# A third seven-product block in each down projection of a two-layer decoder trunk

## The reference

```python
h = rms_norm(x, g_ffn_pre)
f = jax.nn.silu(jnp.einsum('bsd,df->bsf', h, w_gate)) * jnp.einsum('bsd,df->bsf', h, w_up)
x = x + rms_norm(jnp.einsum('bsf,fd->bsd', f, w_down), g_ffn_post)
```

## Time and profile before

| | us |
|---|---|
| runs shown: median (lowest to highest) | 569.01 (568.5 to 569.04) |
| the profiled execution's own time | 568.8 |
| its span, first to last instruction | 567.0 |
| TensorE busy | 559.4 |
| DVE busy | 406.0 |
| ScalarE busy | 301.0 |
| POOL busy | 258.7 |

### The profile page before, as it was taken

The page is one execution under the profiler, slowest core; times in us unless marked ns, Lnnn a source line. Parts: engine busy times, 40 slices in busy tenths (PEclk is TensorE's granted clock), DMA queues, the critical chain, the costliest instruction groups (busy, mean ns, idle before and its releaser), DMA issues.

```text
span 567.0 us, 8931 instructions
## 1 busy us (share of the span) xinstructions
PE 559.4 (99%) x3383; PEld 460.1 (81%) x3383; DVE 406.0 (72%) x529; ACT 301.0 (53%) x428; POOL 258.7 (46%) x451
## 2 busy tenths in 40 slices
PE   8999999999999999999999999999999999999996
PEld 5878878888888888888888878888888888888884
DVE  5799895946755566777797987776848556395783
ACT  7576684664445354354546748564645454345530
POOL 1101001507697787994230000133296797879901
PEclk9999999999999999999999999999999999999999
DMA  8954624538565553547475443526575554644601
GB/s 304 378 203 161 232 94 169 224 133 312 186 223 180 191 213 127 180 174 262 168 266 184 164 168 108 228 76 222 223 260 174 197 202 144 249 148 149 214 10 74
DMA packets 18731, 107.35 MB, mean 189 GB/s; under 512 B 2816, under 2 KB 3072, under 8 KB 7168
## 3 DMA queue, kind: packets, MB, share of 16 engines
q1 hardware_dynamic: 18688, 106.78, 51.6%
HBM read 105.72 MB, written 1.05 MB: 188 GB/s over the span
## 4 chain that ended last, share of the span: by engine, by line
PE 92%; DVE 5%; ACT 1%; issue 1%; POOL 0%; DVEq 0%; POOLq 0%
PE bank L1398 78%; PE bank L1475 4%; PE bank L1413 3%; DVE w_l L919 3%; PE bank L1460 2%; PE bank L1501 2%; PE bank L1528 2%; PE bank L1469 1%; ACT work L725 0%; ACT w_h L642 0%; DVE work L981 0%; DVE work L1003 0%; DVE x L1081 0%; DVE work L1004 0%; DVE work L1074 0%
## 5 line engine op out<-in xcount | busy, mean ns | idle before, releaser
L919 DVE TENSOR_TENSOR w_l<-raw,w_h 128x2048 fp32r<-128x2048 f32 (+1 forms) x90 | 204.4, 2276 | 71.4 <-ACT w_h L642 71.1
L591 POOL COPY work<-work 32x128 f32<-32x128 f32 (+1 forms) x384 | 217.7, 567 | 78.3 <-DVE work L1120 62.5
L1398 PE MATMUL bank<-w_h,actT_h 128*128 128x512 f32 (+1 forms) x568 | 223.9, 394 | 0.3 <-DVE work L981 0.3
L1398 PE MATMUL bank<-w_h,actT_l 128*128 128x512 f32 (+1 forms) x568 | 219.9, 387 | 0.0
L1398 PE MATMUL bank<-w_l,actT_h 128*128 128x512 f32 (+1 forms) x568 | 219.4, 386 | 0.0
L642 ACT ACTIVATE w_h<-raw 128x2048 fp32r<-128x2048 f32 (+1 forms) x90 | 169.6, 1895 | 65.8 <-PE bank L1398 57.5
L1398 PEld LDWEIGHTS bank<-w_h,actT_h 128*128 128x128 f32 x568 | 106.8, 188 | 23.5 <-issue 2.8
L1398 PEld LDWEIGHTS bank<-w_h,actT_l 128*128 128x128 f32 x568 | 106.6, 188 | 22.2
L1398 PEld LDWEIGHTS bank<-w_l,actT_h 128*128 128x128 f32 x568 | 106.9, 188 | 20.0
L576 POOL TENSOR_TENSOR norms<-norms,constants 128x1 f32<-128x1 f32 x8 | 2.7, 342 | 129.0 <-ACT bank L752 129.0
L1475 PE MATMUL bank<-ident,work 128*128 128x128 f32 x228 | 31.4, 273 | 0.0
(11 more groups left out here) (113 smaller groups left out, 566.8 us busy)
## 6 DMA issues: line engine op xcount, KB each, us to landing
raw<-in_w_blocks SPq DMA_DIRECT2D x90, 1024.0 KB, 4.8
gains<-in_b_in SPq DMA_DIRECT2D x8, 256.0 KB, 5.9
raw<-in_w_blocks SPq DMA_DIRECT2D x4, 256.0 KB, 5.5
raw<-in_w_blocks SPq DMA_DIRECT2D x2, 512.0 KB, 8.2
x<-in_x SPq DMA_DIRECT2D x2, 512.0 KB, 10.6
gain_b<-in_g_attn_post SPq DMA_DIRECT2D x2, 512.0 KB, 7.2
gains<-in_g_ffn_pre SPq DMA_DIRECT2D x2, 512.0 KB, 7.4
gain_b<-in_g_ffn_post SPq DMA_DIRECT2D x2, 512.0 KB, 6.5
```

Of the source, the lines that this page charges most:

```text
L591: ins = nc.gpsimd.tensor_copy(crossed[t][32 * j:32 * j + 32, i * n:(i + 1) * n], squares[t][32 * i:32 * i + 32, j * n:(j + 1) * n])
L919: nc.vector.tensor_tensor(w["l"][:, slot(L, b), at:], raw[:, raw_slot(L, b), at:], w["h"][:, slot(L, b), at:].bitcast(F32), ALU.subtract). ...
L1398: ins = nc.tensor.matmul(bank[BANK_OF[name]][:, 0:n], left[s][:, k, :], right[r][:, k, c * BANK:c * BANK + n], start=first and k == 0 and ...
```

## The change

The fast blocks of each down projection become three: the third is rows 4 and 5, the first half of chunk 1, and the plain block of rows 4 is gone. The new order is 35 and 36 plain (rows 6, 8), 37 raw and 38 sum, 39 plain (10), 40 raw and 41 sum, 42 plain (12), 43 raw and 44 sum, 45 to 48 plain (14 to 20). Chunk 1 gets `add_s`, `hi_s` and `lo_s` of its own, over half as many tiles; its second token half keeps 3 tiles of 4. add_squares(0) moves up into the last chunk, add_squares(1) comes before the low part of block 40, add_squares(2) before that of 43. hi_f(4,1) on ScalarE moves behind the high part of block 41, lo_f(4,1) and the last squares on DVE behind its low part, and join_first behind the low part of block 45. The diff, cut to what the prediction speaks of:

```diff
@@ -60,15 +60,14 @@
-FAST = 2
-FAST_CHUNKS = FAST // 2
-BLOCKS += [("down", k, 2, 0, D) for k in (4, 6, 8)]
+FAST = 3
+FAST_CHUNKS = 2
 RAW_AT = []
+BLOCKS += [("down", 6, 2, 0, D)]
 for n in range(FAST):
+    BLOCKS += [("down", 8 + 2 * n, 2, 0, D)]
     RAW_AT += [len(BLOCKS)]
     BLOCKS += [("raw", 2 * n, 2, 0, D), ("sum", 2 * n, 2, 0, D)]
-    if n == 0:
-        BLOCKS += [("down", k, 2, 0, D) for k in (10, 12)]
 FIRST_LATE = len(BLOCKS)
 BLOCKS += [("down", k, 2, 0, D) for k in (14, 16, 18, 20)]
 NB = len(BLOCKS)
...
@@ -368,20 +366,29 @@
             return crossed[t].rearrange("p (i k u b) -> p u k i b", i=4, u=2, b=32)[:, u]
+        def fast_pairs(c):
+
+            return min(2, FAST - 2 * c)
+
         def f_tiles(s, c, t):
-            if c < FAST_CHUNKS:
-                return fT[s][:, 14 * c + 4 * t:14 * c + 4 + 2 * t, :]
-            if c < LAST - 1:
-                at = 14 + 8 * (c - FAST_CHUNKS) + 4 * t
-                return fT[s][:, at:at + 4, :]
+            if c == 0:
+                return fT[s][:, 4 * t:4 + 2 * t, :]
+            if c == 1:
+                return fT[s][:, 14 + 4 * t:18 + 3 * t, :]
+            if c == 2:
+                return fT[s][:, 25 + 4 * t:29 + 4 * t, :]
             if c < LAST:
-                return fX[s][:, 4 * t:4 * t + 4, :]
+                return fX[s][:, 8 * (c - 3) + 4 * t:8 * (c - 3) + 4 * t + 4, :]
             return actT[s][:, 0:f_blocks(c), tokens(t)]
         def s_tiles(s, c):
-            return fT[s][:, 14 * c + 6:14 * c + 14, :]
+            return fT[s][:, 6:14, :] if c == 0 else fT[s][:, 21:25, :]
+
+        def s_raw(c):
+
+            return work_row[:, 0:4 * P * fast_pairs(c)].rearrange("p (s k n) -> p s k n", s=4, n=P)
         def f_part(s, c, t):
...
@@ -491,7 +500,7 @@
                     following = L + 1
-                    place_free(lo_ready, L * NB + RAW_AT[0] + 2)
+                    place_free(lo_ready, L * NB + RAW_AT[2] + 2)
                     sp.dma_start(gain_a, broadcast(g_attn_pre[following], D)).then_inc(gain_a_in, 16)
                     load_bias(following, 0)
                     load_bias(following, 1)
...
@@ -871,13 +880,14 @@
                 after(L, FIRST_DOWN)
                 hi_f(L, FFN_CHUNKS - 2, 0)
                 after(L, FIRST_DOWN + 1)
+                after(L, FIRST_DOWN + 2)
                 hi_f(L, FFN_CHUNKS - 2, 1)
-                for b in range(FIRST_DOWN + 2, RAW_AT[1]):
+                for b in range(FIRST_DOWN + 3, RAW_AT[2]):
                     after(L, b)
                 keep_m1(L)
-                after(L, RAW_AT[1])
+                after(L, RAW_AT[2])
                 hi_f(L, FFN_CHUNKS - 1, 0)
-                after(L, RAW_AT[1] + 1)
+                after(L, RAW_AT[2] + 1)
                 hi_f(L, FFN_CHUNKS - 1, 1)
                 sum_y(L, 1, 0)
                 if L < depth - 1:
@@ -1133,9 +1143,8 @@
                     dve.wait_ge(crossed_in[t], f_count(L, c))
                 if L or c:
                     dve.wait_ge(s_lo_ready, FAST_CHUNKS * L + c)
-                s1, s3, s2, s4 = (s_raw[:, q].rearrange("p k (i b) -> p k i b", b=32) for q in range(4))
-                a11, a12 = f_odd(c, 0, 0), f_odd(c, 0, 1)
-                a21, a22 = f_odd(c, 1, 0), f_odd(c, 1, 1)
+                s1, s3, s2, s4 = (s_raw(c)[:, q].rearrange("p k (i b) -> p k i b", b=32) for q in range(4))
+                a11, a12, a21, a22 = (f_odd(c, t, u)[:, 0:fast_pairs(c)] for t in range(T) for u in range(2))
                 nc.vector.tensor_tensor(s3, a11, a21, ALU.subtract)
                 link(L, nc.vector.tensor_tensor(s1, a21, a22, ALU.add))
                 link(L, nc.vector.tensor_tensor(s2, s1, a11, ALU.subtract))
...
@@ -1303,29 +1312,32 @@
                     swiglu(L, c, 1)
                     if c < FFN_CHUNKS - 1:
                         squares_f(L, c, 0)
+                    else:
+                        add_squares(L, 0)
                     after(L, end)
                     if c < FFN_CHUNKS - 1:
                         squares_f(L, c, 1)
                     if c <= FAST_CHUNKS:
                         lo_s(L, c - 1)
-                first, second = RAW_AT
-                add_squares(L, 0)
+                first, second, third = RAW_AT
                 after(L, FIRST_DOWN)
                 lo_f(L, FFN_CHUNKS - 2, 0)
                 squares_f(L, FFN_CHUNKS - 1, 0)
+                add_squares(L, 1)
                 after(L, FIRST_DOWN + 1)
+                after(L, first)
                 lo_f(L, FFN_CHUNKS - 2, 1)
                 squares_f(L, FFN_CHUNKS - 1, 1)
-                after(L, FIRST_DOWN + 2)
-                add_squares(L, 1)
-                after(L, first)
                 after(L, first + 1)
+                add_squares(L, 2)
                 after(L, first + 2)
+                after(L, second)
+                after(L, second + 1)
                 join_first(L)
-                after(L, first + 3)
-                after(L, second)
+                after(L, second + 2)
+                after(L, third)
                 lo_f(L, FFN_CHUNKS - 1, 0)
-                after(L, second + 1)
+                after(L, third + 1)
                 lo_f(L, FFN_CHUNKS - 1, 1)
                 join_second(L)
                 scale_y(L, 1, 0)
@@ -1382,7 +1394,8 @@
                         for name in names:
                             claim(L, name)
                 if m == "down":
-                    left = {s: f_tiles(s, k0 // 4, t)[:, k0 % 4:k0 % 4 + nk, :] for s in "hl"}
+                    at = k0 % 4 - (1 if (k0 // 4, t) == (1, 1) else 0)
+                    left = {s: f_tiles(s, k0 // 4, t)[:, at:at + nk, :] for s in "hl"}
                 else:
                     left = {s: actT[s][:, k0:k0 + nk, tokens(t)] for s in "hl"}
                 n = min(n, BANK)
@@ -1423,7 +1436,7 @@
                 x11, x12, x21 = (bank[BANK_OF["down", t, q]] for t, q in ((0, 0), (0, 1), (1, 0)))
                 a11, a12 = ({s: f_tiles(s, c, 0)[:, 2 * k + u, :] for s in "hl"} for u in range(2))
                 a22 = {s: f_tiles(s, c, 1)[:, k, :] for s in "hl"}
-                s1, s3, s2, s4 = ({s: s_tiles(s, c)[:, 2 * q + k, :] for s in "hl"} for q in range(4))
+                s1, s3, s2, s4 = ({s: s_tiles(s, c)[:, fast_pairs(c) * q + k, :] for s in "hl"} for q in range(4))
                 b11, b22, b21 = ({s: w[s][:, slot(L, b), q * BANK:(q + 1) * BANK] for s in "hl"} for q in range(1, 4))
                 t1, t3, t2, t4 = ({s: w[s][:, slot(L, b + 1), q * BANK:(q + 1) * BANK] for s in "hl"} for q in range(4))
                 pe.wait_ge(f_lo_ready, F_PARTS.done(L, (c, 1)))
```

More of the change, by code:

```diff
@@ L202, in trunk @@
         actT = {s: sb("actT_" + s, [P, D // P, SEQ], F32R) for s in "hl"}
-        fT = {s: sb("fT_" + s, [P, 38, P], F32R) for s in "hl"}
+        fT = {s: sb("fT_" + s, [P, 33, P], F32R) for s in "hl"}
         raw = sb("raw", [P, RAW, BLOCK])
@@ L241, in trunk @@
         u4, u2, u3, u7 = (work[:, q, :] for q in (0, 2, 3, 2))
-        s_raw = work_row[:, 0:2 * BANK].rearrange("p (s k n) -> p s k n", s=4, k=2)
         ident = sb("ident", [P, P])
@@ L390, in f_from @@
         def f_from(c, t):
-            return f_odd(c, t, 1) if c < FAST_CHUNKS and t == 1 else f_view(c, t)
+            if t == 1 and c < FAST_CHUNKS:
+                return f_odd(c, t, 1) if c == 0 else f_view(c, t)[:, 1:4]
+            return f_view(c, t)
         def sums_of(n):
@@ L682, in hi_s @@
                 act.wait_ge(s_added, FAST_CHUNKS * L + c + 1)
-                nc.scalar.activation(s_tiles("h", c), s_raw.rearrange("p s k n -> p (s k) n"), ACT.Copy
+                nc.scalar.activation(s_tiles("h", c), s_raw(c).rearrange("p s k n -> p (s k) n"), ACT.Copy
                                      ).then_inc(s_hi_ready, 1)
@@ L1146, in lo_s @@
                 dve.wait_ge(s_hi_ready, FAST_CHUNKS * L + c + 1)
-                nc.vector.tensor_tensor(s_tiles("l", c), s_raw.rearrange("p s k n -> p (s k) n"),
+                nc.vector.tensor_tensor(s_tiles("l", c), s_raw(c).rearrange("p s k n -> p (s k) n"),
                                         s_tiles("h", c).bitcast(F32), ALU.subtract).then_inc(s_lo_ready, 1)
```

## The result

The changed kernel takes 572.11 us (571.32 to 572.98, 4 runs) against 568.89 (568.5 to 569.04, 4 runs): 3.2 us slower, ratio 1.005, 95% interval 1.0037 to 1.0063. The forecast was 570.3 with a range of 567.6 to 572.2. The sign and the mechanism came out. The change costs 3.2 us where 1.3 were forecast, a size like that of rival (d), priced at 572.2. The profiled execution took 572.2, its span 570.4.

What follows compares the result with a forecast made beforehand. TensorE, busy 99%, was taken as the bound. Per layer 0.68 us saved and 1.35 of holes give +0.67; two layers, +1.3 on the profiled 568.8, make 570.1, or 570.3 with the median 0.2 higher; range 567.6 to 572.2.

Steps and rivals of the forecast that it cites:

- rival (d): Late start costs too: 0.98 us shift, 0.3 stall at swiglu(5,0), copies holding up DVE 0.6; 1.6 per layer, 572.2 us; chance 0.15.
- Products: TensorE's matmuls: 3377 instead of 3383, saving 0.68 us per layer, 1.36 us in both.
- The lock: DVE instructions with two SBUF inputs keep POOL's copies out, one copy slipping through per instruction; PSUM reads do not.
- FFN chunks: Chunk 1's added sums start swiglu(2,0) 0.59 us late, at 175.21; the delay carries to chunk 5, at cost 0.
- the shift comes out in whole copies: 0.65 or 0.98 us: Delay of the exchange loop carried to chunk 5: 0.65 us would cost 0, 0.98 us would cost 0.3.
- the head of the down stage: First down product at 225.47: swiglu(5,0) ends at 225.28 and, with 0.2 us restart, just meets it, cost 0.
- Down stage, first half: Chunk 4's exchange ends at 247.0, lo(42) at 251.8, block 42 wanted at 251.31: a TensorE hole of about 0.6 us.
- Second half: Chunk 5's exchange ends at 271.4, last join at 274.9; TensorE restarts at 275.1 instead of 274.43, +0.67 us per layer.
- swallows the earlier hole: The wait at the joins absorbs the hole before block 42, since POOL and DVE set the join's time.
- Loads: 46 loads of 1 MB per layer as before, reordered; block 48's starts at 260.7 and takes 4.8 us.
- The low part of block 48 is not the last thing: End of down stage: hi(48) ends at 267.5, DVE reaches it at 268.1, before exchange (5,1) ends at 271.4.
- Layers alike: Layer 1 repeats layer 0's positions, so +0.67 us per layer makes +1.3 us for two layers.

## Why the prediction was right or wrong

**Products.** Right: 3377 matmuls, and with the holes away 1.1 us less (0.0019 of the time, interval 0.0010 to 0.0028; 1.36 was reckoned).

**The lock.** Right, and shown: by the copies with PSUM and SBUF inputs, and by 2.4 us measured for 2.35.

**FFN chunks, the term that was mis-sized.** swiglu(2,0) was reckoned at 175.21 and started at 175.17; add_s(1) took 1.07 us (reckoned 1.06). But then "the shift comes out in whole copies: 0.65 or 0.98 us" and I took 0.65. That was against my own sum: a start 0.59 late and 0.37 for lo_s(1) are 0.96, which is the larger step. Exchange 2 lasted 19.48 us and not 19.02, and the next starts are 1.0 us late (200.13 for 199.12, 222.52 for 221.53). I also put the cost at the head of the down stage at nothing: swiglu(5,0) ended at 225.62, and TensorE, wanted at 225.46, started at 225.88, holes of 0.42 and 0.93. There was no cover left, so an error could go one way only, and the forecast should have carried the larger step in its likeliest number.

What this is worth has to be read where TensorE waits last, at the joins. They hang on POOL's and DVE's chain from 222.52 on, which does not pass through the hole at the head, so that hole is covered by their wait (this is read from the rows of TensorE, POOL and DVE; no run separates it). What counts is the later start of exchange 4. It is 0.34 us more than reckoned in each layer and another 0.51 in layer 1. The pair of exchanges (49.59, reckoned 49.2) adds 0.4 a layer, TensorE's quicker restart takes 0.15 off, and the products behind the join's hole, set a little apart, add 0.15. In both layers together this is 2.0 us, the difference between the forecast's +1.3 and the span's +3.4. Only in the run handed over in chunks 4 and 5 alone, where no join is waited for, does the head of the stage cost 1.3 us by itself.

Rival (d) had the larger step, at 0.33 a layer, and 0.6 for copies that hold DVE up; its sum of 572.2 was met, but by other sizes, which is luck. How much DVE is held up by copies was not tried alone: the low parts of whole blocks that fall into these two exchanges last 2.29 to 2.40 us in layer 0, so at most 0.11 each.

**Down stage, first half.** Right: exchange (4,*) was reckoned to end at 247.0 and hi_f(4,1) starts at 247.57, late by 0.34 of the larger shift and 0.2 more. The hole before block 42 was put at 0.6 and is 0.56. That it fits is in part luck: lo(42) ended at 252.33 and not at 251.8, and TensorE, itself held up at the head of the stage, wanted it at 251.83 and not at 251.31.

**Second half.** Right in kind. Exchange (5,1) was reckoned to end at 271.4, hi_f(5,1) starts at 272.14: 0.34 us later by its start, 0.4 by lasting longer. One rate was misread: the earlier trace rows give 0.25 us for a copy of 32x64 (11 in 2.80, 6 in 1.50) and not 0.27, under 0.1 us in the sum. The last join was put at 274.9 and ended at 275.67. TensorE restarts 0.05 after it and not 0.2. It passes at 275.72 and not at 274.43, +1.29 where +0.67 was reckoned. That this "swallows the earlier hole" is shown, for the hole before block 42, by the run with hi_f(4,1) later: one hole gone, the other grown, the same time.

**Loads.** Half right. "The low part of block 48 is not the last thing" holds, but closely: the load came at 267.15 and not at 265.5, ScalarE had waited 2.51 us, and DVE 0.17 more (the bracket of DVE's row at 269.11). In no run does TensorE wait for a low part in the down stage other than that of block 42.

**Layers alike.** Wrong: layer 1's first hole is 0.93 and not 0.42. The 0.51 us between them come from two exchanges ahead of the down stage: that of chunk 0 lasts 18.71 us in layer 1 and 18.40 in layer 0, that of chunk 3 lasts 19.20 and 19.00. The first 0.31 is about one copy at the free pitch, and it stands ahead of everything that the change adds to the layer. It is no rule: in the runs with half the copies, without weight sums and with hi_f(4,1) later, which do the same work up to there, TensorE's wait for swiglu(5,0) is 0.2 to 0.3 us in both layers. Why a copy fell on the other side in this execution stays open.

## What to carry to other kernels

When two engines contend for SBUF, count an engine's time twice: where it stands on its own queue, and in every exchange of the other that it falls into. Price it as its length less the one copy that slips through per instruction, and look for a loop through both engines that is already slower than the bottleneck, because there the price is carried on to the end of the loop. And where the cover that is left is smaller than the step in which a delay comes, take the step; a piece of the contended work on a third engine with idle time, which DVE's work did not hold up, was worth more here than the one other order that was tried.

## What the runs showed of the hardware that was not expected

ScalarE carries a 32x128 block to other partitions in 0.308 us, as fast as POOL's free pitch of 0.325, and was not held up by DVE's work beside it: the longest of its 64 copies in the run that hands over chunks 2 to 5 took 0.311 us, and the four from 241.40 on ran in 1.27 us beside a low part that DVE had begun at 241.41. After a hole TensorE's next products start 0.31 to 0.34 us apart once or twice before the 0.227 returns, 0.1 to 0.15 us a hole. TensorE started 0.05 us after the join that released it ended, and 0.26 after swiglu(5,0), so one restart figure does not fit all.
